# VectorE makes a weight tile's remainder 6 blocks behind ScalarE's rounding in place of 2, in the stages with small products

## What is computed

```python
for layer in range(2):
    x = x + 0.5 * swiglu(rmsnorm(x), w_in, w_out)
    x = x + (attn_lru_mixer, deltanet_mixer)[layer](rmsnorm(x))
    x = x + cross_attention(rmsnorm(x), rmsnorm(mem), wq, wkv, wo)
    x = x + 0.5 * swiglu(rmsnorm(x), w_in2, w_out2)
for i in range(4):
    u = rmsnorm(h)
    y = (retention, conformer_conv, gla)[i % 3](u)
    h = h + rmsnorm(y)
    h = h + rmsnorm(sq_relu_mlp(rmsnorm(h), w_up, w_down))
```

## Time and profile before

| | |
|---|---|
| median of 3 runs | 2608.23 us (2608.0 to 2609.23) |
| the profiled execution | 2607.9 us |
| its span, first to last instruction | 2606.1 us |
| PE busy in the span | 2561.8 us |
| VectorE busy | 1779.8 us |
| ScalarE busy | 1381.8 us |
| mean granted clock of PE | 0.996 |
| remainders on VectorE (line 1074) | 835 of 1222 ns |
| roundings on ScalarE (line 2192) | 835 of 1053 ns |

### The profile page before, as it was taken

The page is one execution under the profiler, slowest core; times in us unless marked ns, Lnnn a source line. Parts: engine busy times, 40 slices in busy tenths (PEclk is TensorE's granted clock), DMA queues, the critical chain, the costliest instruction groups (busy, mean ns, idle before and its releaser), DMA issues. The chain is left out here.

```text
span 2606.1 us, 49997 instructions
## 1 busy us (share of the span) xinstructions
PE 2561.8 (98%) x21566; PEld 2477.3 (95%) x21566; DVE 1779.8 (68%) x2269; ACT 1381.8 (53%) x1839; POOL 0.2 (0%) x4
## 2 busy tenths in 40 slices
PE   9999999999999999999999999999999999999998
PEld 9999999999998999999999999799989999999998
DVE  7668767656768756776766875478455885766774
ACT  5546655454468465545456544364465554456443
POOL 0000000000000000000000000000000000000000
PEclk9999999999999999999999999999999999999999
DMA  7554546555553344655544555645543555544553
GB/s 271 181 190 160 177 146 203 194 191 194 194 166 119 117 151 146 203 194 185 187 145 162 188 194 182 174 166 195 194 138 122 187 193 191 177 152 166 177 195 131
DMA packets 135163, 456.02 MB, mean 175 GB/s; under 512 B 20512, under 2 KB 26272, under 8 KB 134816
## 3 DMA queue, kind: packets, MB, share of 16 engines
q1 hardware_dynamic: 134800, 452.69, 52.6%
q10 hardware_dynamic: 144, 0.14, 0.0%
HBM read 450.15 MB, written 2.62 MB: 174 GB/s over the span
## 5 line engine op out<-in xcount | busy, mean ns | idle before, releaser
L289 PE MATMUL B<-R,WH 128*128 128x256 f32 x10432 | 2025.5, 279 | 15.0 <-DVE WL L1079 5.1
L289 PEld LDWEIGHTS B<-R,WH 128*128 128x128 f32 x10432 | 1658.0, 189 | 29.9 <-issue 15.7
L1074 DVE TENSOR_TENSOR WL<-SL,WH 128x1024 fp32r<-128x1024 f32 x835 | 1004.8, 1222 | 576.1 <-ACT WH L2192 574.7
L289 PE MATMUL B<-R,WL 128*128 128x256 f32 x4480 | 1237.9, 277 | 0.0
L2192 ACT ACTIVATE WH<-SL 128x1024 fp32r<-128x1024 f32 x835 | 861.3, 1053 | 455.0 <-PE B L289 430.2
L289 PEld LDWEIGHTS B<-R,WL 128*128 128x128 f32 x4480 | 845.1, 189 | 0.0
L289 PE MATMUL B<-RB,WH 128*128 128x256 f32 x1984 | 547.7, 276 | 0.2 <-DVE WL L1074 0.2
L289 PE MATMUL B<-RB,WL 128*128 128x256 f32 x1728 | 477.0, 276 | 0.0
L289 PEld LDWEIGHTS B<-RB,WH 128*128 128x128 f32 x1984 | 372.4, 188 | 0.5 <-DVE WL L1074 0.4
L289 PEld LDWEIGHTS B<-RB,WL 128*128 128x128 f32 x1728 | 324.3, 188 | 0.0
L289 PE MATMUL B<-WH,R 128*128 128x512 f32 x480 | 157.0, 398 | 0.0
(11 more groups left out here) (310 smaller groups left out, 1482.1 us busy)
## 6 DMA issues: line engine op xcount, KB each, us to landing
SL<-in_w SPq DMA_DIRECT2D x835, 512.0 KB, 3.3
CP<-in_cp SPq DMA_DIRECT2D x5, 768.0 KB, 4.8
BIG<-c_hp SPq DMA_DIRECT2D x12, 284.0 KB, 5.3
c_hp<-BIG SPq DMA_DIRECT2D x4, 288.0 KB, 4.7
PG<-c_hp SPq DMA_DIRECT2D x4, 284.0 KB, 5.0
PG<-in_mem SPq DMA_DIRECT2D x1, 1024.0 KB, 6.3
PK<-in_pk SPq DMA_DIRECT2D x1, 614.5 KB, 8.9
XG<-in_xT SPq DMA_DIRECT2D x1, 512.0 KB, 7.4
```

Source lines behind the costliest of these rows:

```text
L289: return p.matmul(o, left, right, start=first, stop=final, skip_group_check=True)
L1074: v.tensor_tensor(WL[t % NRAW][:, :], SL[t % NRAW][:, :], WH[t % NSPL][:, :].bitcast(F32), ALU.subtract).then_inc(s_lo, 1)
```

## The change

In the same stages the shift becomes 6 blocks. Since the calls of one stage's last tile then fall into the next stage, `walk` gets two additions: if the stage before was one of these too, its last tile is made at block 2 of this one; and where the next stage isn't one of these, the tile that is left over is made behind the last block.

```diff
+        NAMES = list(ST)
+
         def behind(name):
-            return 2 if name[0:2] in ("dn", "xv", "xk", "g.", "r0", "r3") and name[-1] not in "oqk" or name in ("dn.k", "dn.q", "xq0", "xq1") else 0
+            return 6 if name[0:2] in ("dn", "xv", "xk", "g.", "r0", "r3") and name[-1] not in "oqk" or name in ("dn.k", "dn.q", "xq0", "xq1") else 0
...
                 for x, (j, k) in enumerate(st.order):
                     b, x0 = st.block + x * st.width - behind(name), x - behind(name) // st.width
-                    if b and b % 4 == 0 and x0 >= skip and x0 not in ahead(name):
+                    if b and b % 4 == 0 and (x0 >= skip and x0 not in ahead(name) or x0 < 0 and behind(NAMES[NAMES.index(name) - 1])):
                         lo(b // 4 + 4)
                     yield j, k
                     if n is not None and not st.outer and (j, k) == (0, 3):
                         add_squares(n, 3)
+                if behind(name) and not behind(NAMES[NAMES.index(name) + 1]):
+                    for b in range(st.done(st.groups - 1) - behind(name), st.done(st.groups - 1)):
+                        if b % 4 == 0:
+                            lo(b // 4 + 4)
```

## The result

The median after the change is 2616.53 us (8 runs, 2613.83 to 2619.6) against 2608.47 for the kernel before beside it (8 runs, 2607.14 to 2609.23). The ratio is 1.0032, with a 95% interval from 1.0022 to 1.0043: slower by 8.1 us (5.7 to 11.2 by the interval), more than the 0.2% that can be told from no change. The profiled execution took 2615.86 us, its span is 2614.1, 8.0 more than before.

A forecast was written before the change was run, and what follows sets the result against it. PE was taken to bound the kernel; 8.1 (retentions) + 2.4 (xk1b) - 1.0 (dn.k) + 0.3 (g.r) = 9.8 us, giving 2617.7, or 2618.0 as median; own range 2614 to 2622, 8 in 10 for 2611.5 to 2623.

The forecast's parts named there:

- What bounds the kernel: Whole kernel: PE busy 2561.8 of 2606.1 us, so only PE's idle stretches and its pace can move the time.
- The rule of slots: Touched stages: slots keep their places but hold tile t-1; late if the next tile's earlier slot ends after PE arrives.
- Part 1: Retentions' v1 stages: tile 423 and its counterpart come behind K's rotation, late by 1.9, cost 2.25 us each.
- Part 2: Retentions' gate stages: last tiles of g2 and g3 late by 0.08 and 1.04, cost 0.4 and 1.4 us per retention.
- rival (a): VectorE, freed from waits for ScalarE, reaches slots earlier, so margins hold: 2606.5 us; chance 0.13 together with no effect.
- Part 3: xk1b, last stage before dn.o: tiles 302, 303, 304 late, 305 in time; net cost 2.4 us.
- Part 4: Entry into dn.k: the empty slot lets the additions of squares end before PE arrives; gain 1.0 us.
- Part 5: End of g.r: left-over tile 639 ahead of `gate(3)` delays the work behind it; cost 0.3 us.
- What should cost nothing: Delta rule's tiles 271 and 280 late by 0.1 and 1.7 inside existing L1564 waits; xk0, DMA, ScalarE's order: 0.
- Clock: Half-speed stretches of 3.41 us, 1.7 us each: one gained, one lost, net 0, with ends -1.7 and +5.1.

The follow-up runs named there:

- Experiment 6: Offset 6 only in the retentions' gate stages, 2 elsewhere, VectorE's rounding wait kept in g2; 2609.74 us against 2608.62 for the kernel before, ratio 1.0007.
- Experiment 5: Offset 6 only in the retentions' gate stages g0 to g3, 2 elsewhere; 2608.17 us against 2608.62 for the kernel before, ratio 0.9998.
- experiments 6 and 8: 8: offset 6 in the retentions' value stages alone, tiles 423 and 727 made after three quarters of K's last rotation operation; one execution, 2612.48 us.

## Why the prediction came out

The forecast was 2618.0, the measurement 2616.53: right in sign, in nearly all places and in size. But two of its terms were off by 3.2 us each, in opposite directions (the clock in v1, and g3), so that the total came this near is in part luck.

- **What bounds the kernel: right.** Idle PE and PE's pace were all that moved; of the 54 us less waiting of VectorE, PE got 1.2 in dn.k and 1.2 in each g3. One reading was wrong: the list of PE's waits does have a long wait for a weight remainder, 4.82 us for the program's first tile (L1079, 5.1 in all). The change doesn't touch it (4.9 after).
- **The rule of slots: right.** Each late tile stood in the slot that had been the next one's: 423, 439, 443, 302 to 304, 271 and 280.
- **Part 1: right in the wait, short by the clock.** 2.25 was forecast for each v1, 2.26 is the wait and the restart. The falls behind them were named, but only one was counted, and as balanced by one lost.
- **Part 2: g2 right (0.4 and 0.44), g3 wrong (+1.4 and -0.25).** The step that failed is the sentence against rival (a), that the pieces ahead of the late slots start "not behind a rounding". For the rotation and for the heads of xk1b that is so. For `gated` it isn't: it waits for ScalarE's work on g2's last scaling, and that scaling stood behind a remainder that waited 1.65 for its rounding. After the change the wait is 0.52. The forecast for g3 was off by 1.65. Experiment 6 put the wait back, and 1.2 of this came back (-0.25 to +0.96). The rest of the error is a PE wait that I had not set against the lateness: the 0.72 for the head's sum (L1940) in the same stage, which the late tile covers in part (0.25 is left in experiment 6) and which is gone where the chain comes sooner. So what rival (a) says, VectorE freed from a wait for ScalarE reaches the slot earlier, was true in g3, and in no other place with a late tile.
- **Part 3: right.** +2.40 against 2.4; alone +2.37. The waits are 0.18, 1.11 and 0.86; the forecast's terms were 0.45, 1.43 and 1.2 with the restart in each.
- **Part 4: right in mechanism and size.** PE's wait of 0.97 is gone and dn.k alone shows -1.20:

```profile
754.50 0.42 DVE L1131 TENSOR_TENSOR PG<-PG 128x256 f32<-128x256 f32 x1
755.35 2.36 DVE L1076 TENSOR_TENSOR WL<-SL,WH 128x1024 fp32r<-128x1024 f32 x2 [0.41 <-ACT WH L2198]
```

  The additions end at 754.92, ahead of the rounding that they had waited for in the earlier trace rows. The other 1.4 of the -2.61 is a half-speed stretch that was absent. Experiment 5 doesn't touch dn.k and had the stretch absent too, with -1.43; so it isn't the change's.
- **Part 5: the term is there, and something else hides it.** PE waits 0.42 for the last head's remainder (0.14 before), the 0.3 forecast. Its wait for the first head's is 1.00 in place of 1.35. But experiments 6 and 8, which leave g.r and g.o as they were, have 1.01 and 1.00 as well, so this one comes and goes by the execution.
- **What should cost nothing: right.** Tiles 271 and 280 are late, by waits of 0.14 and 0.89, and PE's waits for L1564 behind them fell from 0.76 and 2.19 to 0.32 and 1.07. The lateness lies inside them.
- **Clock: net 0 in number, right by chance.** Both profiled executions have five half-speed stretches within the stages. Two new ones belong to the change (6 of 6, against 8 of 14 for a wait only 0.1 shorter). The two that vanished, in dn.k and dn.z, come and go in kernels that don't touch them. The forecast's 0 should have been +3.1, with the vanished ones as noise. Its price of 1.7 for each holds only where nothing else waits: 1.57 in v1, 1.43 in dn.k, but 0.6 to 0.7 in dn.z and 0.45 in dn.q, where PE meets other waits instead. The one stretch that the forecast counted as lost, dn.q's, would have given back 0.45.

The half-speed stretch of dn.q was present in 8 of 14 traces behind the same wait. What the prediction called unseen, a fall that one execution has and another hasn't, is now seen. The Trainium skill ("TensorE: Matmul & The Clock Gate", Part 1) says that the monitor runs freely and that the point of transition therefore varies from run to run. It says so of the rise at a kernel's start; these traces show the like for falls in mid-kernel. The page's description of the low level as that of an idle array doesn't cover these cases: in front of both falls in v1, PE was busy 1.42 and 1.41 of 3.41 us. The stretch of dn.k follows no such wait at all: in the kernel before, the nearest one ends 7.4 us ahead of it, and PE was busy for all of the 3.41 us ahead of 764.98, nearly all of it with 32 products of 16 columns:

```profile
761.29 3.64 PE L289 MATMUL B<-PK,H 128*128 128x16 f32 x32
```

The same 32 products stand there in experiment 5, which has no half-speed stretch in dn.k.

Left open: why waits of 2.17 to 2.20 in dn.z go with half speed in 6 of 9 traces only (in the kernel before it begins 0.2 us ahead of the wait's end), while 1.99 in v1 always did. PE's other work around them differs (many 128-column products there, 512-column ones here), and that was not tried apart.

## What to carry to other kernels

An in-order engine that serves two customers has a slot order, and what a change of lag does is read tile by tile: the slot's end against the consumer's arrival, at the places where long work lies between two slots. When a wait on that engine goes, follow the chain forward from it through the other engines to the next slot before calling it free or useless; here 54 us of such waits went, and what of them reached PE was 1.2 us in each retention and 1.2 us in dn.k. And look at urgent small work that stands behind a remainder with time to spare: putting the remainder behind that work at the entries of the normed stages gave 6.5 us, where moving all remainders lost 8.

## What the runs showed of the hardware

- The restart behind a late operand cost 0.27 us beyond the wait, for waits of 0.37, 0.86, 1.46 and 1.73 in r0.v1 and r3.v1.
- A PE wait of 1.99 inside work that is otherwise dense was followed by 3.41 us at half speed in 6 of 6 places and cost 1.57 more; waits of 0.86, 1.46 and 1.73 in the same places (one, one and two) were not. Shortening the wait from 1.99 to 1.73 saved 1.8 there.
- Half speed came without a wait too: in dn.k, in 11 of 14 traces, within or right behind 32 products of 16 columns in a row.
- The same wait of 1.85 to 1.88 had the fall behind it in 8 of 14 executions. A comparison of two single profiles can be off by several such stretches in stages that are the same in both. What one was worth differs with what waits behind it: 1.43 us in dn.k, 0.6 to 0.7 in dn.z, 0.45 in dn.q.
